# Large expert turns: the extra 32 tokens multiplied with unsplit weights in four column groups, and constant products in four waits of TensorE

## The reference, cut to what matters

```python
logits = (x @ w_router + b_router)
top_v, top_i = lax.top_k(logits, TOP_K)            # TOP_K = 2 of N_EXPERTS = 8
probs = jax.nn.softmax(top_v, axis=-1)
gates = sum(one_hot(top_i, N_EXPERTS) * probs)
for e in range(N_EXPERTS):
    out = out + gates[..., e:e + 1] * swiglu(x, w_gate[e], w_up[e], w_down[e])
# swiglu(x, g, u, d) = (silu(x @ g) * (x @ u)) @ d ; g, u: 1024 x 2816, d: 2816 x 1024
```

## Time and profile before

| | us |
|---|---|
| median of 3 runs | 1990.87 (1989.12 to 1992.35) |
| the profiled execution, whole | 1984.89 |
| its span, first to last instruction | 1983.1 |
| from the first product of turn 0 to the end of its last | 165.7 |
| a small turn, from its clearing product to the next turn's | 99.9 |
| turn 7, the same stretch as turn 0 | 165.8 |

### The profile page before, as it was taken

How to read it: one execution, slowest core, us unless ns; L and a number is a source line. 1 busy time by engine, 2 the same in 40 slices (tenths; PEclk the granted TensorE clock), 3 DMA queues, 4 the chain that set the end, 5 groups by cost and what they waited for, 6 DMA issues and landing times.

```text
span 1983.1 us, 28034 instructions
## 1 busy us (share of the span) xinstructions
PE 1878.6 (95%) x10353; PEld 1604.9 (81%) x10354; DVE 1482.1 (75%) x2119; ACT 1066.3 (54%) x1206; POOL 136.5 (7%) x159
## 2 busy tenths in 40 slices
PE   7999999899998999999889999999999999999993
PEld 7899899799987989899766678888888888886672
DVE  6997686755536999667576668888888888886665
ACT  4452754543324444474444456767777776765442
POOL 1110000000001020000020001020202020201000
PEclk9999999899999999999989999999999999999997
DMA  7553344344443563444456569898989898996522
GB/s 268 203 215 143 138 151 144 109 168 149 149 141 116 191 229 136 149 149 150 149 211 250 199 233 339 335 382 331 374 331 380 337 375 333 366 346 241 210 106 87
DMA packets 118613, 446.91 MB, mean 225 GB/s; under 512 B 10384, under 2 KB 10384, under 8 KB 118016
## 3 DMA queue, kind: packets, MB, share of 16 engines
q1 hardware_dynamic: 112288, 424.45, 58.1%
q0 software_dynamic: 6240, 21.33, 3.2%
HBM read 435.68 MB, written 12.67 MB: 226 GB/s over the span
## 4 chain that ended last, share of the span: by engine, by line
PE 42%; issue 3%; DVE 3%; ACT 1%; DMA 1%; SPq 0%; DVEq 0%; POOLq 0%; POOL 0%; ACTq 0%
PE psum L1996 11%; PE psum L1997 11%; PE psum L1998 11%; PE psum L2003 3%; PE psum L2002 3%; ACT wph L616 1%; PE psum L1736 1%; PE psum L2059 1%; DVE wpl L622 1%; DVE hT L1674 0%; DMA x<-out_acc 0%; DMA out_acc<-arena,rows_out 0%; DVE arena L1663 0%; PE psum L2062 0%; DVE x L1164 0%
## 5 line engine op out<-in xcount | busy, mean ns | idle before, releaser
L622 DVE TENSOR_TENSOR wpl<-e_ring,wph 128x2048 fp32r<-128x2048 f32 x269 | 606.9, 2289 | 85.5 <-ACT wph L616 84.5
L616 ACT CAST wph<-e_ring 128x2048 fp32r<-128x2048 f32 x269 | 501.7, 1903 | 119.6 <-PE psum L1998 66.7
L574 DVE TENSOR_TENSOR wl<-ring,wh 128x1024 fp32r<-128x1024 f32 x234 | 285.3, 1223 | 208.1 <-ACT wh L568 207.4
L1750 PE MATMUL psum<-xTh,wh 128*128 128x320 f32 x1184 | 375.3, 317 | 31.6 <-DVE xTl L1266 11.0
L1751 PE MATMUL psum<-xTl,wh 128*128 128x320 f32 x1184 | 369.9, 312 | 0.0
L1752 PE MATMUL psum<-xTh,wl 128*128 128x320 f32 x1184 | 369.7, 312 | 0.0
L568 ACT CAST wh<-ring 128x1024 fp32r<-128x1024 f32 x234 | 243.9, 1046 | 138.6 <-PE psum L1771 71.2
L1996 PE MATMUL psum<-wph,xe 128*128 128x512 f32 (+1 forms) x768 | 293.6, 382 | 2.8 <-issue 2.4
L1997 PE MATMUL psum<-wph,xe 128*128 128x512 f32 (+1 forms) x768 | 289.1, 376 | 0.0
L1998 PE MATMUL psum<-wpl,xe 128*128 128x512 f32 (+1 forms) x768 | 288.7, 376 | 0.0
L1750 PEld LDWEIGHTS psum<-xTh,wh 128*128 128x128 f32 x1184 | 225.7, 191 | 40.0 <-DVE wl L574 15.7
(11 more groups left out here) (327 smaller groups left out, 2528.5 us busy)
## 6 DMA issues: line engine op xcount, KB each, us to landing
e_ring<-experts SPq DMA_DIRECT2D x264, 1024.0 KB, 6.4
ring<-stream SPq DMA_DIRECT2D x274, 512.0 KB, 3.2
lnp<-rows POOLq DMA_DIRECT2D x4, 1024.0 KB, 6.1
x<-x POOLq DMA_DIRECT2D x3, 512.0 KB, 5.8
arena<-x0T SPq DMA_DIRECT2D x2, 640.0 KB, 5.9
o_a<-arena POOLq DMA_DIRECT2D x2, 540.0 KB, 7.6
o_k<-arena POOLq DMA_DIRECT2D x2, 512.0 KB, 7.0
o_v<-arena POOLq DMA_DIRECT2D x2, 512.0 KB, 8.8
```

The lines of the kernel that those rows point to most:

```text
L574: dve.tensor_tensor(wl[:, q % SPLITS, :], ring[:, u % SLOTS, :], wh[:, q % SPLITS, :].bitcast(F32), ALU.subtract).then_inc(lo_done, 1)
L616: act.copy(wph[:, SLOT_OF[m % NPOS], :], ring_place(m).rearrange("p u c -> p (u c)")).then_inc(hi_e, 1)
L622: dve.tensor_tensor(wpl[:, s, :], ring_place(m).rearrange("p u c -> p (u c)"), wph[:, s, :].bitcast(F32), ALU.subtract).then_inc(lo_e, 1)
L1750: pe.matmul(out, h[:, k], hi[:, k], start=(k == 0), stop=False)
```

## The change

- **B tokens on raw weights.** `into_b` multiplies the unsplit B tokens (`xe_b`, fp32) with the raw weights in `e_ring`, in four groups of 32 columns of the array, one for each 128 hidden columns. Output: 32 tokens x 4 groups on 128 partitions, 128 columns wide, instead of 32 (+32) partitions and 512 columns. `down` does it too, with four groups of 256 output columns. There are no high and low parts of B any more, so ACT and DVE have one sigmoid and two small products per chunk, and ACT scales the B output alone.
- **Ring.** As PE now reads the raw weights in large turns, SP loads in a large turn only when PE is through with the slot's former position (`mm_e`). In small turns it goes by `lo_e` as before. SP reads `nv` and `size` for this, and issues six loads ahead of the turns (one for each slot) in place of ten.
- **B rows of the scatter.** 128 pieces of 256 numbers (`group_at`) in place of 32 of 1024; `turn_done` is gone.
- **Constant products.** `idle_products` puts 9, 5, 6 and 8 fp32 products of 160 columns, whose output nobody reads, ahead of four waits of PE: before the first block, after the router weights have landed, ahead of the "pos" products, and ahead of the gather.

```diff
 MEAN_AFTER = 2
+IDLE_FIRST, IDLE_ROUTER, IDLE_POS, IDLE_GATHER = 9, 5, 6, 8
 TAIL, HEAD = T, T + NSAMP
...
 
+FIRST_LOADS = [m for m in range(LOAD_AHEAD) if SLOT_OF[m] not in SLOT_OF[:m]]
+TURN_LOADS = sorted((m for m in range(2 * NPOS) if 0 <= before_in_slot(m) < NPOS and SLOT_OF[m % NPOS] in SLOT_OF[:m]),
+                    key=before_in_slot)
+LAST_LOADS = [m for m in TURN_LOADS if m < NPOS]
+
+assert sorted(LAST_LOADS + FIRST_LOADS) == list(range(NPOS)) and len(TURN_LOADS) == NPOS
+assert sorted(m - NPOS for m in TURN_LOADS if m >= NPOS) == FIRST_LOADS
 assert len(SLOT_OF) == NPOS
...
 
-            for m in range(LOAD_AHEAD):
+            for m in FIRST_LOADS:
                 r = RING_ROW[SLOT_OF[m]]
-                if SLOT_OF[m] in SLOT_OF[:m]:
-                    sp.wait_ge(lo_e, before_in_slot(m) + 1)
-                elif r < SLOTS // 2:
+                if r < SLOTS // 2:
                     for u in (n_units - SLOTS + 2 * r, n_units - SLOTS + 2 * r + 1):
                         sp.wait_ge(lo_done, plan.split[u] + 1)
                 else:
                     sp.wait_ge(mm_done, split_steps[-1])
                 load(m, 0)
 
-            def expert(i, e, last):
-
-                for m in range(LOAD_AHEAD, last):
-                    sp.wait_ge(lo_e, i * NPOS + (before_in_slot(m) + 1))
+            def expert(i, e, loads, big):
+
+                for m in loads:
+                    if big:
+                        sp.wait_ge(mm_e, i * NPOS + (before_in_slot(m) + 1))
+                    else:
+                        sp.wait_ge(lo_e, i * NPOS + (before_in_slot(m) + 1))
                     load(m, e + 1 if m >= NPOS else e)
 
             def free_after(i):
@@ -703,18 +712,22 @@
                     sp.wait_ge(lo_e, i * NPOS + before_in_slot(m) + 1)
                     sp.sem_inc(e_full[SLOT_OF[m % NPOS]], 16)
 
-            with sp.Fori(0, NE - 1) as i:
-                expert(i, i, LOAD_AHEAD + NPOS)
-            expert(NE - 1, NE - 1, NPOS)
             sp.wait_ge(nv_ready, 1)
             nv = sp.value_load(nvi[0:1, 0:1], min_val=NE, max_val=2 * NE)
+            with sp.Fori(0, NE - 1) as i:
+                n = sp.value_load(size[0:1, bass.ds(i, 1)], min_val=0, max_val=1)
+                with sp.If(n > 0):
+                    expert(i, i, TURN_LOADS, True)
+                with sp.Else():
+                    expert(i, i, TURN_LOADS, False)
+            expert(NE - 1, NE - 1, LAST_LOADS, True)
             with sp.If(nv > NE):
-                for m in range(NPOS, NPOS + LOAD_AHEAD):
-                    sp.wait_ge(lo_e, (NE - 1) * NPOS + before_in_slot(m) + 1)
+                for m in FIRST_LOADS:
+                    sp.wait_ge(mm_e, (NE - 1) * NPOS + before_in_slot(NPOS + m) + 1)
                     load(m, 0)
                 with sp.Fori(NE, 2 * NE - 1) as i:
-                    expert(i, i - NE, LOAD_AHEAD + NPOS)
-                expert(2 * NE - 1, NE - 1, NPOS)
+                    expert(i, i - NE, TURN_LOADS, True)
+                expert(2 * NE - 1, NE - 1, LAST_LOADS, True)
                 free_after(2 * NE - 1)
             with sp.Else():
                 free_after(NE - 1)
...
-                pool.wait_ge(turn_done, i + 1)
                 pool.wait_ge(scur_done, i + 1)
                 pool.wait_ge(out_moved, i * 32 + 48)
                 pool.sem_inc(scatter_begun, 1)
                 pool.indirect_dma_start(out_acc, bass.IndirectOffsetOnAxis(ap=rows_out[:, 0:1], axis=0), ys_a, None,
                                         bounds_check=T - 1, oob_is_err=False, compute_op=ALU.add)\
                     .then_inc(out_moved, 16)
-                pool.indirect_dma_start(out_acc, bass.IndirectOffsetOnAxis(ap=rows_out[0:CAP_B, 1:2], axis=0),
-                                        ys_b[0:CAP_B], None,
-                                        bounds_check=T - 1, oob_is_err=False, compute_op=ALU.add)\
+                pool.indirect_dma_start(out_acc.rearrange("t (g c) -> (t g) c", g=GROUPS),
+                                        bass.IndirectOffsetOnAxis(ap=rows_out[:, 1:2], axis=0), ys_b, None,
+                                        bounds_check=GROUPS * T - 1, oob_is_err=False, compute_op=ALU.add)\
                     .then_inc(out_moved, 16)
...
                     if big:
-                        act.copy(gate_b[0:CAP_B, 0:w], psum[CAP_B:2 * CAP_B, BANK_X, 0:w])
+                        rows = w // GROUPS
+                        act.activation(sg_b[0:rows], psum[0:rows, BANK_X, 0:P], ACT.Sigmoid)
                     act.activation((sg_e if big else h_b)[:, 0:w], psum[:, BANK_G, 0:w], ACT.Sigmoid)\
                        .then_inc(sig_done, 1)
-
...
                     if big:
-                        dve.tensor_tensor(gate_b[0:CAP_B, 0:w], psum[0:CAP_B, BANK_X, 0:w], gate_b[0:CAP_B, 0:w],
-                                          ALU.add)
+                        rows = w // GROUPS
+                        dve.tensor_tensor(sg_b[0:rows], psum[0:rows, BANK_X, 0:P], sg_b[0:rows], ALU.mult)
                     sg = sg_e if big else h_b
                     dve.tensor_tensor(sg[:, 0:w], psum[:, BANK_G, 0:w], sg[:, 0:w], ALU.mult)\
                        .then_inc(gated_done, 1)
@@ -1651,13 +1652,9 @@
                     if j == 0:
                         dve.wait_ge(out_moved, i * 32 + 48)
                     if big:
-                        dve.wait_ge(hb_ready, i * NJ + (j + 1))
-                        dve.tensor_tensor(gate_b[0:CAP_B, 0:w], gate_b[0:CAP_B, 0:w], sg_b[0:CAP_B, 0:w], ALU.mult)
-                        dve.tensor_tensor(h_b[0:CAP_B, 0:w], psum[0:CAP_B, BANK_T, 0:w], h_b[0:CAP_B, 0:w], ALU.add)\
-                           .then_inc(hb_sum, 1)
-                        dve.tensor_tensor(h_e[:, 0:w], psum[:, BANK_U, 0:w], sg_e[:, 0:w], ALU.mult)
-                        dve.wait_ge(hb_sum, i * NJ + (j + 1))
-                        dve.tensor_tensor(h_b[0:CAP_B, 0:w], h_b[0:CAP_B, 0:w], gate_b[0:CAP_B, 0:w], ALU.mult)\
+                        rows = w // GROUPS
+                        dve.tensor_tensor(h_b[0:rows, 0:P], psum[0:rows, BANK_T, 0:P], sg_b[0:rows], ALU.mult)
+                        dve.tensor_tensor(h_e[:, 0:w], psum[:, BANK_U, 0:w], sg_e[:, 0:w], ALU.mult)\
                            .then_inc(hid_done, 1)
                     else:
...
 
+            def idle_products(out, n):
+
+                for _ in range(n):
+                    pe.matmul(out[:, 0:CAP], ones[:], iota[:], start=True, stop=True)
+
             def turn_x(l, name, n):
 
...
 
-                def into_b(kind, j, b, at):
-
-                    n = len(CHUNKS[j])
-                    h, low = split_of(kind, CHUNKS[j][0], n, at)
+                def into_b(kind, j, b):
+
+                    weight = [ring_place(AT[kind, f])[:, u] for f in CHUNKS[j] for u in range(2)]
                     for k in range(KT):
-                        ks = slice(P * k, P * k + P)
-                        ins = packed(b, slice(0, 2 * P * n), xe[:, k, BOTH_B], xe[:, k, HI_B], h[:, :, ks],
-                                     low[:, :, ks], k == 0, k == KT - 1)
-                    ins.then_inc(mm_e, n)
+                        for g, w in enumerate(weight):
+                            ins = pe.matmul(psum[CAP_B * g:CAP_B * g + CAP_B, b, 0:P], xe_b[:, k],
+                                            w[:, P * k:P * k + P], start=(k == 0), stop=(k == KT - 1),
+                                            skip_group_check=True)
+                    ins.then_inc(mm_e, len(CHUNKS[j]))
 
                 def clear_down():
 
                     for c in range(2):
                         pe.matmul(psum[:, BANK_D + c, :], zero[:, 0:P], zero[:], start=True, stop=False,
                                   skip_group_check=True)
-                        if big:
-                            pe.matmul(psum[0:2 * CAP_B, BANK_DB + c, :], zero[:, 0:2 * CAP_B], zero[:], start=True,
-                                      stop=False, skip_group_check=True)
+                    if big:
+                        pe.matmul(psum[:, BANK_DB, 0:D_OF], zero[:, 0:P], zero[:, 0:D_OF], start=True, stop=False,
+                                  skip_group_check=True)
 
                 def down(f, at, hidden):
 
                     h, low = split_of("down", f, 1, at)
                     for u in range(2):
-                        th = hidden[:, 2 * (f % 2) + u]
+                        th, th_b = hidden[0][:, 2 * (f % 2) + u], hidden[1][:, 2 * (f % 2) + u]
                         final = f == FT // 2 - 1 and u == 1
                         for c in range(2):
                             cs = slice(512 * c, 512 * c + 512)
                             ins = triple(psum[:, BANK_D + c, :], th[:, HI_A], th[:, LO_A], h[:, u, cs], low[:, u, cs],
                                          False, final)
-                            if big:
```

(29 more changed lines are left out.)

82 lines of the change are left out of this document (29 added, 53 removed).

## The result

| | before | after |
|---|---|---|
| median of 4 runs | 1989.99 us (1988.71 to 1992.35) | 2007.93 us (2004.88 to 2009.66) |
| span of the profiled execution | 1983.1 us | 2003.0 us |
| mean granted clock | 0.982 | 0.970 |

The change makes the kernel slower by 0.87% (ratio 1.0087, 95% interval 1.007 to 1.0105). The forecast was 1979.9, the range 1957 to 1998: wrong in sign and outside the range.

What follows compares the result with a forecast made beforehand. PE's own work was taken as the bound in large turns. Turns -11.1, clock +4.5, end -2.3 and constant products -2.1 summed to -11.0, from 1990.87 to 1979.9 us; range 1957 to 1998.

Steps and rivals of the forecast that it cites:

- PE's work, -22.8 a large turn: Large turns: 32.3 us of products, clearing and transposes saved, less 9.5 for 34 column-group excursions at 0.28.
- Stalls, 20.6 and 15.7 us: Turns 0 and 7: PE waits because a slot's load and split follow its use in series, less 1.4 idle now.
- A: Chunk 0 of a large turn: a 10.0 us load-and-split chain against 5.0 of PE work, stall 5.0.
- C: Three middle rounds of a large turn: PE has 8.3 or 8.4 us against 10.0, stall 1.6 each, 4.8 together.
- D: Last chunk of a large turn, with a narrow gate: PE has 5.6 us of work, stall 4.4.
- E: End of turn 0 only, next turn's load ahead of the last `hidden_lo`: 10.3 against 5.4 us, stall 4.9.
- Clock, +4.5: Half clock behind five stalls over 4 us, 1.7 us each: between 0 and 8.5, the middle taken.
- Turns 0 to 1 and 1 to 2, +1.0: Turn 1 finds its first splits later by some 1 us; SP's new reads and branches cost nothing, at most some us.
- Constant products, -2.1: Waits ahead of the turns: start 0, router +1.3, pos -1.8, gather -1.6; +1.3 net if the clock falls anyway.
- 1: Rival: going into column groups and out costs nothing, most of 9.5 us per large turn returns; 1966 us, chance 0.18.
- 2: Rival: the ring does not bind, loads land and split in PE's time; 52.8 us less, 1938 us, chance 0.07.
- 3: Rival: late landings, 1.4 us more in each of 13 chains; 1998 us, decides from 5.9 us, chance 0.13.

Runs made afterwards that it cites:

- number 9: Changed kernel plus constant products in PE's waits of the large turns: 1994.70 us, ratio 1.0028 to the kernel before.
- Experiment 2: Kernel before plus 816 empty PE instructions in the large branch of its loop: 2026.30 us, ratio 1.0185 to the kernel before.
- number 1: Changed kernel plus a branch prefetch hint on the closing jump of PE's turn loop: 2004.86 us, ratio 1.0074 to the kernel before.
- Numbers 6 and 7: Changed kernel, raw products first, one PE program for large and small turns; with constant products 1968.58 us (0.9905), without 1969.79 us (0.9902).
- number 8: Shared-program, raw-first kernel with constant products, one SP wait instead of two before each large-turn load: 1959.89 us, ratio 0.9861 to the kernel before.
- number 3: Changed kernel without the constant products in the four waits: 1993.98 us, ratio 1.0036 to the kernel before.
- number 4: Kernel before plus only the constant products in the four waits: 1984.17 us, ratio 0.9977 to the kernel before.

## Why the prediction was wrong, point by point

- **PE's work, -22.8 a large turn: right.** Turn 0 of number 9 has 154.35 us busy, of which 32 constant products at 0.30 us are 9.6, and 2% of half clock some 3. What is left, 141, is 23 under the 164.5 of the earlier trace rows. The rounds of four groups ran as priced: from the start of an `into_b` of eight k to the next product it is 1.88 us, 0.235 each.
- **Stalls, 20.6 and 15.7 us: right as idle time (20.4 and 14.8), too small as a chain.** In turn 0 A was 4.5 with 0.9 behind it, C 2.5, 1.8 and 2.0, D 4.7, E 4.0. But part of PE's time between them ran at half clock. Near full clock, in number 9, waits (14.1 and 9.0) and fillings (9.6 each) come to 23.7 us in turn 0 and 18.6 in turn 7. One chain C of the changed kernel, from the timeline:

```profile
1071.84 0.64 PE L2038 MATMUL psum<-e_ring,hT_b 128*32 128x256 f32 x8
```
```profile
1078.26 1.90 ACT L624 CAST wph<-e_ring 128x2048 fp32r<-128x2048 f32 x1 [0.90 <-DMA e_ring<-experts]
```
```profile
1080.19 2.29 DVE L630 TENSOR_TENSOR wpl<-e_ring,wph 128x2048 fp32r<-128x2048 f32 x1 [0.51 <-ACT wph L624]
1082.40 0.68 DVE L1667 TENSOR_TENSOR hT<-psum,hT 128x512 fp32r<-128x512 f32 x1
```

  From the end of the product that frees the place (1072.5) to the end of `hidden_lo` (1083.1) it is 10.6 us for my 10.0; the load lands some 5.5 us after its issue, for 5.0. The 4.4 us that the prediction cites beside it come from a formula which that section gives for transfers issued by GpSimd; SP issues these.
- **Clock, +4.5: too small, and the wrong way to count.** The half-clock stretches of turn 0 add up to 23 us and those of turn 7 to 14, which is up to 12 and 7 us of PE's time. Number 9 takes 8 and 5 us of that back, and gains 3.2 and 0.3 us. Inside a turn in which PE waits for load and split, stalls and clock are not to be added: a slow PE shortens the wait. The two turns come to +3.0 us for -7.6, a miss of 10.6. By number 9 some 6.0 of it are the longer chain (unless a filling outlasted its wait), 3.5 the clock that filling gives back, and up to 5.1 the half clock left even then, less the 4.5 that were forecast: some 10 of the 10.6.
- **Turns 0 to 1 and 1 to 2, +1.0: the step that failed.** I wrote that "SP's new reads and branches cost nothing", which held for SP, and priced no instruction supply for PE at all, at 588 records more in its loop. Measured are +15.9 us, in two gaps of 6.25 and 6.30 where there were 2.36 and none, and half clock behind each (0.51 over 6.03 us, 3 us lost, and here PE is the bound, so it is lost). Of the 15.9, 10.2 are idle time and the rest is half clock. This is 14.9 of the 30.9 us between the forecast -11.0 and the +19.9 of the profiled spans; the turns are 10.6, the stretch ahead of them 5.9, the end -0.5. Experiment 2 makes the first gap by code length alone, in 1 it goes with the fetch, and 6 to 8 have neither. For the second gap the evidence is the branch record, the fetched blocks, and the 9 us that go with it in 3 and 9.
- **Constant products, -2.1: right in sign in the kernel before (-4.6), not seen in the changed one.** Its first expert product came 3.8 us later. 1.82 of that is a gap of "issue" ahead of turn 0 (1.84 in number 3, none before); the wait for the router's weights was 4.0 us for 1.7, but 3.6 in number 3, 3.1 in number 8 and 2.4 in number 4, so it varies by itself. What else of it belongs to the change isn't settled. Numbers 6 and 7 show no difference either.
- **The end, -2.3: right, -2.7.** The last product before ended at 1951.24 and not at 1951.7, so 5.4 us to POOL's first scatter became 2.7.
- **The rivals.** 1: no, going into column groups and out again costs 0.20 us around each group (starts 0.32 and 0.34 apart where two rounded products are 0.233 apart), for my 0.28. 2: no, PE does wait. 3, late landings: 5.2 and 5.4 us median in turns 0 and 7, under the 5.9 from which it would decide; right on the side, not by its mechanism. 4: no. (1.4 us in each of 13 chains is 18, so its sum is +7, not +8; the 1998 is right.)

Left open: what decides whether the second jump is long, and why 3 and 9 seem to have it more rarely than the changed kernel.

## What to carry to other kernels

Count an engine's instructions in a loop whose branches alternate, in its records and not in the source, before adding to it: an fp32 product counts four. Once the loop outgrows what the engine keeps, a far jump can cost a gap that no data explain. If a buffer's last reader changes, put that reader first among those that work on it; the order was worth 28 us here between profiled executions and 38 between medians. Do not add a clock penalty to a stall in a stretch that another chain bounds.

## What the runs showed of the hardware

- A closing jump of PE costs 0.2 us while its target is kept, and 4.6 to 7.8 us when it isn't; two misses in a row left PE idle for 11 us (experiment 2). The transfer is about half of it at most: a block takes 0.9 to 1.4 us alone as a rule, and 1.1 to 2.7 when two go together.
- The end of the large branch costs 3.3 to 6.0 us where it is long (0.2 in the last turn before and in number 1). It shows the less the more products PE has queued: before, 4.4 us of products covered 2.6 of the 5.0.
- Ahead of the turns, one block of 16,384 bytes is fetched for each 255 recorded instructions of PE.
- SP has a limit too, at a much smaller size, with blocks of 8,192 bytes: with 33 waits more in its large branch it stood for 7.7 us behind two branches at each later turn boundary (5.1 and 2.5). Only turn 1 became longer by it (110.6 for 100.7 us); the small turns behind it took 100.7 us with and without.
- 816 empty instructions on PE cost 13.5 us in a large turn, though only 12 stand together.
